# A two-stack transformer kernel: steps of the second stack's mixer placed between the tiles of its input projection

## The reference

```python
hx = modulate(rmsnorm_2(xs, mix_norm[l]), m_x, 1)
hc = modulate(rmsnorm_2(cs, mix_norm[l]), m_c, 1)
px = hx @ w_in[l]
if last:
    pc_kv = hc @ w_in[l][:, OFF_KV:]
else:
    pc = hc @ w_in[l]
    pc_kv = pc[..., OFF_KV:]
...
f = fourier_mix(proj[..., OFF_F:OFF_CB])                # fft2 over tokens and 64 channels, real part
cv = conv_mix(proj[..., OFF_CB:OFF_CC], proj[..., OFF_CC:OFF_CX], proj[..., OFF_CX:OFF_Q], conv_w)
...
kv_lat, k_rope = p_kv[..., :KV_LORA], p_kv[..., KV_LORA:]
kv = (rmsnorm_2(kv_lat, kv_norm) @ w_ukv).reshape(b, n, MLA_HEADS, QK_NOPE + V_DIM)
...
q = (rmsnorm_2(q_lat, q_norm) @ w_uq).reshape(b, n, MLA_HEADS, QK_NOPE + QK_ROPE)
```

## Time and profile before

| | |
|---|---|
| median of three runs | 2722.24 us |
| the profiled execution: its time | 2721.82 us |
| the profiled execution: its span | 2720.0 us |
| TensorE, VectorE, ScalarE busy | 2507.4, 1846.3, 1099.7 us |
| projection of layer 0, tiles 3 to 13 | 1350 to 1410 us |
| mixer of layer 0 | 1410 to 1443 us |
| projection of layer 1, tiles 3 to 13 | 2347 to 2390 us |
| mixer of layer 1 | 2390 to 2408 us |

### The profile page before, as it was taken

One profiled execution on the slowest core, in us unless ns is written; L12 is line 12 of the kernel. 1 busy time (PEld: TensorE's weight loads), 2 busy tenths in 40 slices (PEclk: granted clock), 3 DMA queues, 4 the chain that ended last, 5 costly groups with the idle time before them and its releaser, 6 DMA issues.

```text
span 2720.0 us, 37566 instructions
## 1 busy us (share of the span) xinstructions
PE 2507.4 (92%) x15010; PEld 2147.0 (79%) x15010; DVE 1846.3 (68%) x3136; ACT 1099.7 (40%) x1695; POOL 53.3 (2%) x56
## 2 busy tenths in 40 slices
PE   5889999866899799999987899999999999978998
PEld 4849999754799778888875588888888888866997
DVE  2647999644566667787945677676876666866666
ACT  4475447722454532222514452222442222544543
POOL 1010000021000000000000000000000000000000
PEclk8999999988999899999998999999999999988999
DMA  7877996522466546655322036555445554422663
GB/s 260 244 227 202 282 279 181 155 93 78 129 183 186 148 124 171 176 164 166 101 51 72 8 98 166 155 163 157 138 133 157 140 151 124 120 76 60 182 185 109
DMA packets 632563, 407.59 MB, mean 150 GB/s; under 512 B 27751, under 2 KB 588614, under 8 KB 631366
## 3 DMA queue, kind: packets, MB, share of 16 engines
q1 hardware_dynamic: 631712, 404.94, 51.8%
q10 hardware_dynamic: 678, 0.25, 0.0%
HBM read 404.09 MB, written 1.05 MB: 149 GB/s over the span
## 4 chain that ended last, share of the span: by engine, by line
PE 83%; DVE 8%; ACT 4%; DMA 2%; issue 1%; SPq 1%; ACTq 0%; POOL 0%; DVEq 0%; POOLq 0%
PE ps L1562 71%; PE ps L1584 2%; PE ps L1599 1%; PE ps L569 1%; PE ps L833 1%; DMA raw<-in_attn_w_in 1%; PE ps L1336 1%; DVE w_lo L1900 1%; PE ps L843 1%; PE ps L1311 1%; DVE p L1405 1%; DVE stat L1395 1%; DVE tmp L2100 0%; PE ps L1323 0%; DVE ada_acc L1917 0%
## 5 line engine op out<-in xcount | busy, mean ns | idle before, releaser
L1742 ACT CAST w_hi<-raw 128x1024 fp32r<-128x1024 f32 (+3 forms) x557 | 554.7, 997 | 1210.4 <-PE ps L1562 1174.0
L1562 PE MATMUL ps<-h_hi,w_hi 128*128 128x258 f32 (+2 forms) x2952 | 969.4, 328 | 27.2 <-DVE h_lo L2109 13.7
L1562 PE MATMUL ps<-h_lo,w_hi 128*128 128x258 f32 (+2 forms) x2952 | 964.5, 327 | 0.0
L1562 PE MATMUL ps<-h_hi,w_lo 128*128 128x258 f32 (+2 forms) x2952 | 963.6, 326 | 0.0
L1900 DVE TENSOR_TENSOR w_lo<-raw,w_hi 128x1024 fp32r<-128x1024 f32 (+3 forms) x557 | 644.9, 1158 | 256.9 <-ACT w_hi L1742 253.9
L1562 PEld LDWEIGHTS ps<-h_hi,w_hi 128*128 128x128 f32 x2952 | 561.3, 190 | 82.5 <-issue 26.5
L1562 PEld LDWEIGHTS ps<-h_lo,w_hi 128*128 128x128 f32 x2952 | 560.8, 190 | 46.7
L1562 PEld LDWEIGHTS ps<-h_hi,w_lo 128*128 128x128 f32 x2952 | 561.2, 190 | 45.4
L1562 PE MATMUL ps<-a_hi,w_hi 128*128 128x256 f32 (+1 forms) x1056 | 354.6, 336 | 0.5 <-DVE a_lo L1955 0.5
L1562 PE MATMUL ps<-a_lo,w_hi 128*128 128x256 f32 (+1 forms) x1056 | 353.2, 334 | 0.0
L1562 PE MATMUL ps<-a_hi,w_lo 128*128 128x256 f32 (+1 forms) x1056 | 353.2, 334 | 0.0
(11 more groups left out here) (350 smaller groups left out, 2249.0 us busy)
## 6 DMA issues: line engine op xcount, KB each, us to landing
raw<-in_ffn_w_in SPq DMA_DIRECT2D x264, 512.0 KB, 4.6
ada_raw<-in_w_mod SPq DMA_DIRECT2D x120, 512.0 KB, 3.9
raw<-in_ffn_w_out SPq DMA_DIRECT2D x96, 512.0 KB, 5.0
ada_raw<-in_ada_w SPq DMA_DIRECT2D x40, 512.0 KB, 5.4
wide_rows<-in_ada_w SPq DMA_DIRECT2D x40, 512.0 KB, 5.0
raw<-in_ffn_w_out SPq DMA_DIRECT2D x48, 384.0 KB, 3.6
raw<-in_gdn_w_in SPq DMA_DIRECT2D x33, 512.0 KB, 4.1
raw<-in_w_in SPq DMA_DIRECT2D x26, 512.0 KB, 3.9
```

Of the source, the lines that this page charges most:

```text
L1562: last = mm(ps[0:m, slot, 0:n], w[:, slot, k * P:k * P + m], v[:, s0 + k, c0:c0 + n], start=(k == 0 and w is w_hi and v is hi), stop=(k == ...
L1742: nc.scalar.copy(w_hi[:, slot, 0:n], raw[:, slot, 0:n]).then_inc(s_hi, 1)
```

## The change

`MIXER_STEPS` lists for each layer the order of the 14 tiles and behind which tile each mixer step stands; the results still go to the same blocks of `proj2`. The query latents (8, 9, 10) come first in both layers. In layer 0 the key-value latents and the key follow (11, 12, 13), in layer 1 four more tiles of one stream, then those three, then the last four. The mixer's functions become steps (`mixer_step_tensor`, `mixer_step_scalar`, `mixer_step_vector`) called inside the loops over the tiles; on VectorE the step stands ahead of the result copy of its tile, on ScalarE behind the cast and the epilogue. The squares move from VectorE to ScalarE; `fm` gets four buffers instead of two. Behind the last tile stay: the second convolution's gate, the splits of the mixed rows into two parts, and the later half of the token passes. In layer 1 the norm of the query latent and that of the key-value latent now have a logarithm and exponential each, where one pair of table loads served both.

```diff
+MIXER_STEPS = (
+    dict(order=(8, 9, 10, 11, 12, 13, 0, 1, 4, 6, 2, 5, 7, 3), kv=3, kr=5, f=6, q_sums=6, kv_sums=6, q_rstd=7, kv_rstd=7,
...
+    dict(order=(8, 9, 10, 0, 1, 4, 6, 11, 12, 13, 2, 5, 7, 3), kv=7, kr=9, f=3, q_sums=5, kv_sums=10, q_rstd=6, kv_rstd=11,
...
+        parts = ((0, 7, T), (7, 10, 2 * T), (10, 14, T)) if layer else ((0, 14, 2 * T),)
         st += [("norm", "both", ("mla", layer), 2 * T),
-               Linear("mixer_in", ("w_in_2", layer), KD, 11, own, loads=loads[:11], first=0, early="h"),
-               Linear("mixer_in", ("w_in_2", layer), KD, 3, 2 * T, loads=loads[11:], first=11),
+               *(Linear("mixer_in", ("w_in_2", layer), KD, b - a, n, loads=[loads[i] for i in order[a:b]], first=a, early=None if a else "h")
+                 for a, b, n in parts),
...
+            if t == at_["turn"]:
+                pe.wait_ge(s_evac, g0 + at_["kr"] + 1)
+                pe.wait_ge(event("latent_rstd"), 2 * layer + 1)
+                mm(ps[:, 7, 0:T], const("swap2"), proj2[:, 13, 0:T], start=True, stop=True).then_inc(event("k_rotated"), 1)
+            if t == 12:
+                for i in range(n_s):
+                    fourier_tokens(pe, layer, i)
+            if t == 13:
+                pe.wait_ge(event("latent_rstd"), 2 * layer + 2)
+                pe.wait_ge(event("k_roped"), layer + 1)
+                for i in range(n_s, 2 * n_s):
+                    fourier_tokens(pe, layer, i)
...
+        def mixer_step_scalar(act, lin, t):
...
+            if t in latent_squares(layer):
...
+                nc.scalar.activation(sq[:, e % 2, 0:n], proj2[:, at_["order"][t], 0:n], ACT.Square).then_inc(event("latents_squared"), 1)
+            sums = [("q_rstd", n_s * T, 384, ssq, 7, 1), ("kv_rstd", 2 * T, 256, rstd, 6, 2)]
+            sums = [s[1:] for s in sums if at_[s[0]] == t]
+            for n, width, r, bank, count in sums:
+                act.wait_ge(event("latent_sums"), 2 * layer + count)
+                last = nc.scalar.activation(r[:, 0:n], ps[:, bank, 0:n], ACT.Ln, scale=1.0 / width, bias=const("eps"))
...
+                    if lin.kind == "mixer_in":
+                        mixer_step_tensor(pe, lin, lin.more["first"] + j)
...
-                elif st[0] == "mixer":
-                    mixer_tensor(pe, st)
```

More of the change, by code:

```diff
@@ L1184, in mixer_scalar @@
[L1184 to L1191, removed]
@@ L1202, in latent_parts, with conv_out @@
-        def latent_parts(n_s):
[L1204 to L1208, removed]
+            hi = mixed_rows(st)[0]
+            act.wait_ge(s_tile, tiles_before(st))
+            def conv_out(f):
+                act.wait_ge(event("conv_mixed"), 2 * layer + f + 1)
+                nc.scalar.copy(hi[:, 2 + f, 0:n_s * T], cv[:, f, 0:n_s * T]).then_inc(event("conv_hi"), 1)
@@ L1212, in mixer_vector @@
             layer, n_s = st[1], 2 - st[1]
-            tokens = n_s * T
-            b, nb = 4 * mixer_base(st), 2 * mixer_base(st)
+            hi, lo = mixed_rows(st)
             dve.wait_ge(s_evac, tiles_before(st))
[L1217 to L1224, removed]
@@ L1277, in mixer_vector, with conv_lo @@
-            last.then_inc(s_h, 4 * n_s)
+            conv_gated(layer, 1)
+            for k in range(*MIXER_STEPS[layer]["parts"].get(13, (0, 0))):
+                latent_lo(dve, layer, k)
+            dve.wait_ge(event("conv_mixed"), 2 * layer + 2)
+            def conv_lo(f):
+                dve.wait_ge(event("conv_hi"), 2 * layer + f + 1)
+                return V.tensor_tensor(lo[:, 2 + f, 0:n_s * T], cv[:, f, 0:n_s * T], hi[:, 2 + f, 0:n_s * T].bitcast(F32), ALU.subtract)
+            conv_lo(0)
@@ L1422, in mla_vector @@
                     V.tensor_tensor(mixed_rows(st)[1][d], ps[:, 6 + b % 2, 0:T], mixed_rows(st)[0][d].bitcast(F32), ALU.subtract).then_inc(s_h, 1)
-        def lat_blocks(lin):
-            i = next(n for n, s in enumerate(stages) if s is lin)
-            total = 0
-            for s in stages[:i]:
-                if not isinstance(s, Linear) and s[0] == "mixer":
-                    total += 4 + 3 * (1 if s[1] else 2)
-            return total
         block = stack.enter_context(nc.Block())
@@ L1620, in waits @@
                 if src == "lat":
-                    total = lat_blocks(lin)
+                    layer = lin.weight[1]
+                    total = 10 * layer + 3 * (2 - layer) + (4 if lin.kind == "key_value" else 0)
                     return lambda k: (event("lat_written"), total)
@@ L1808, in _ @@
                         epilogue(st, j)
+                        if st.kind == "mixer_in":
+                            mixer_step_scalar(act, st, st.more["first"] + j)
                         norm, late = late_parts(st, j)
@@ L2152, in _ @@
                             angles()
+                        if st.kind == "mixer_in":
+                            mixer_step_vector(dve, st, st.more["first"] + j)
                         epilogue(st, j)
```

218 lines of the change are left out of this document (123 added, 95 removed).

## The result

| | before | changed |
|---|---|---|
| median, timed side by side | 2723.19 us (2720.78 to 2724.53, four runs) | 2698.79 us (2694.61 to 2701.40, four runs) |
| the same in a later comparison | 2723.65 us (2720.77 to 2726.34, nine runs) | 2698.87 us (2697.87 to 2701.49, four runs) |
| profiled execution: span, time | 2720.0, 2721.82 us | 2699.6, 2701.36 us |

A forecast was written before the change was run, and what follows sets the result against it. TensorE, carrying 83% of the chain that ended last, was taken as the bound. Layer 0's 22.4 us plus layer 1's 0.5 make 22.9 off the median 2722.24: 2699.3, rounded 2699 us, range 2693 to 2705.

The forecast's parts named there:

- Layer 0, 22.4 us: Layer 0's gain: query 20.1 us sooner plus 2.3 us from the full clock; bounds 20 to 23.5.
- the breaks: Cost of small steps interrupting projection matmuls: 0.1 us each, 7 in layer 0 and 6 in layer 1; bounds zero and 0.2.
- The wait ahead of tile 7, 8.6 us: Layer 1: TensorE waits 8.6 us for the last normed blocks before the first tile of both streams.
- ScalarE's detour: Layer 1: two table loads, a logarithm and an exponential ahead of the last two h_hi; without their cost, wait 6.5 us.
- The low clock behind it, 2.0 us: Layer 1: after the wait TensorE runs at the lower clock level for a while, losing 1.8 to 2.6 us, taken as 2.0.
- Query 54 us after tile 4: Layer 1: from tile 4 to the first query matmul takes 54 us, the query starting at 2407.7, as before.
- Layer 1, plus 0.5 us: Layer 1's gain: 0.8 us at the query tiles less some 0.3 for breaks; bounds a 2.5 loss to a 5 gain.
- The table loads: ScalarE: each load counted as 1.28 us without drain; the skill's 2.66 us would lengthen the wait by 2.8, giving 2702.
- layer 1 did not pay: Rival 1: tile 7's wait does not form or stays short, layer 1 gives 12 us, time 2688; chance 0.06.
- rival 2: New waits cost more than counted: layer 0 gives 20 us, layer 1 loses 3, time 2705; chance 0.17.
- layer 0 lost nothing in its tail: Rival 4: layer 0's last convolution and mixed-row splits hold the query back by 8 us, time 2707; chance 0.05.
- the full grant held for 70 us: Rival 3: a lower clock throughout the interleaved stretches makes the kernel slower than before, 2732; chance 0.03.

The follow-up runs named there:

- l1_only: Layer 1 as in the changed kernel, layer 0 as in the kernel before: 2723.26 us, ratio 1.0003 to the kernel before.
- l0_conv_tail: Changed kernel with layer 0's second convolution (3.0 us of VectorE) moved from under the last projection tile to behind it: 2701.01 us, ratio 0.9918.
- busy: Changed kernel with 17 matmuls, whose results nothing reads, filling TensorE's wait ahead of layer 1's tile 7: 2698.57 us, ratio 0.991.
- shift1_late: Changed kernel with one more one-stream tile ahead of layer 1's two-stream tiles, and the query norm's logarithm and exponential one tile later: 2693.99 us.
- shift2: Changed kernel, layer 1's two-stream tiles two places later, query norm's logarithm and exponential later, last two key-value latent parts behind the last tile: 2694.27 us.
- shift1: Changed kernel with one more one-stream tile and its feature pass ahead of layer 1's first two-stream tile: 2694.38 us, ratio 0.9891.
- l0_only: Layer 0 as in the changed kernel, layer 1 with the old tile order and old mixer: 2702.13 us, ratio 0.9925.
- changed_again: The changed kernel timed once more, beside later variants: 2698.87 us.

## Why the prediction was right, point by point

The places and causes were right. That the time was hit to 0.2 us is luck: layer 0 gave 0.5 us more than forecast and layer 1 some 0.6 us less, the two misses cancel, and medians with an interval of 5 us to either side could not have told 2699 from 2695 or 2703.

- **Layer 0, 22.4 us.** Measured 22.9 (126.51 to 103.58), and 126.45 in `l1_only` for 102.96 to 103.92 in the nine executions with the new order. The query was to come 20.1 us sooner and came 20.7 sooner. The step that was too large is the breaks, 0.1 us each: eleven tiles of 5.445 us (four of them from 1352.27 to 1374.05) are 59.9, the steps 12.5, together 72.4 of the 72.43 measured. The row of the first query matmul starts some 0.2 us early (0.41 us ahead of the next, where the later ones are 0.23 apart), so the seven breaks cost up to 0.2 us in all, where 0.7 was counted. The clock's 2.3 us held: query to rotation took 31.15 for 33.34.
- **No wait in layer 0.** Right, with 3.9 us of room, and 1.9 with 3 us more of VectorE in the tail (`l0_conv_tail`).
- **The wait ahead of tile 7, 8.6 us.** Measured 8.37 to 8.39. Both parts were right in kind: taking ScalarE's detour away leaves 6.47, where 6.5 was written as the bound without it.
- **The low clock behind it, 2.0 us.** It was 2.5 (`busy`), and 2.3 to 2.5 in the four executions with this order against the 5.53 us that tile 7 takes at the full clock: the upper end of the 1.8 to 2.6 given. This is the term that was mis-sized. The low level lasted up to 5.25 us (2351.60 to 2356.85), where 3.6 to 5.2 had been read from the kernel before.
- **Query 54 us after tile 4.** 54.45, 54.21, 54.42 and 54.40 us in four executions; the forecast was 0.2 to 0.5 too low, which is about what that term lacks. The 0.5 us of wait at query tile 3 was there (0.53).
- **Layer 1, plus 0.5 us.** In the profiled execution it was 1.1 us of loss. The other three executions with this order give 77.27 to 77.86 us, for 77.47 and 77.96 with the old one: on the mean 0.1 us of loss, so neither gain nor loss can be told. Of the 1.6 us missing in the profiled execution, half a microsecond is the clock term. The other step that failed is that the loads behind the mixer follow "at the same pace". The wait ahead of the rotation was 2.40 us before and 3.52 after: the last key-value results stand on VectorE behind weight parts of the output projection, these behind casts, and these behind loads. `l1_only`, whose wait was 2.40 us as before, took 77.27 us, 0.2 less than before. ScalarE in the changed kernel:

```profile
2404.31 1.05 ACT L1783 CAST w_hi<-raw 128x1024 fp32r<-128x1024 f32 x1 [1.21 <-DMA raw<-in_w_out]
2406.92 1.05 ACT L1783 CAST w_hi<-raw 128x1024 fp32r<-128x1024 f32 x1 [1.56 <-DMA raw<-in_w_out]
```

and VectorE:

```profile
2408.01 1.23 DVE L1943 TENSOR_TENSOR w_lo<-raw,w_hi 128x1024 fp32r<-128x1024 f32 x1 [0.78 <-ACT w_hi L1783]
2409.15 0.68 DVE L2086 COPY kv<-ps 128x512 f32<-128x512 f32 x1
```

Over both layers of the eleven profiled executions this wait was 2.40 to 2.81 us with the old order (four times, mean 2.6) and 2.40 to 3.52 with the new one (eighteen times, mean 2.9). That the query tiles now run into these loads sooner fits it, but the scatter of one order is as large as the difference, and no run held the loads apart, so this cause is argued and not shown.
- **The table loads.** The activation behind a load of 1.28 us starts 0.01 us after it, twice in the rows above (0.02 in the earlier trace rows), and the load itself starts 0.02 us behind the cast ahead of it, so no drain stands on either side. The Trainium skill, "ScalarE: Activation LUTs", section "What ACT_TABLE_LOAD costs", would add 1.38 us of drain to each; the wait would then be 11 us, and it is 8.4. The 1.28 us of the trace decide.
- **The rivals.** None came whole: layer 1 did not pay, of rival 2 only the low level of 5 us came, layer 0 lost nothing in its tail, and the full grant held for 70 us with seven groups of small steps in it.

## What to carry to other kernels

Work moved from a tail into a stretch where the bounding engine is full costs its own length there and saves the whole chain of the tail; count the engines that make the inputs of the tiles whose order changes with it, for a reordering can bring a hidden producer to the front. In such a place each microsecond taken off the new wait pays until the next queue shows, here the weight parts behind VectorE's tail, so look at what the other engines still do behind the last tile before trying for more.

## What the hardware showed

- **A short idle time lowers the clock too, and after a delay.** After 2.72 us without work (`shift1_late`) TensorE came back at the full clock, 0.23 us from the second matmul to the third, and then fell to 1.2 GHz, some 0.43 us apart, for eight of them:

```profile
2350.24 0.47 PE L1604 MATMUL ps<-h_hi,w_hi 128*128 128x512 f32 x1 [2.72 <-DVE h_lo L2154]
2350.55 0.41 PE L1604 MATMUL ps<-h_hi,w_lo 128*128 128x512 f32 x1
2350.78 0.61 PE L1604 MATMUL ps<-h_lo,w_hi 128*128 128x512 f32 x1
2351.19 0.63 PE L1604 MATMUL ps<-h_hi,w_hi 128*128 128x512 f32 x1
...
2354.18 0.42 PE L1604 MATMUL ps<-h_hi,w_lo 128*128 128x512 f32 x1
2354.43 0.39 PE L1604 MATMUL ps<-h_lo,w_hi 128*128 128x512 f32 x1
```

  The same happened after 3.45 us in `shift2`. The low level cost 2.3 to 2.5 us after 8.4 us of idle time, 1.7 after 6.47 us, and 2.0 and 1.6 after 4.65 and 2.72 us (the three wide tiles took 18.4 and 18.05 us, for 16.4 in `shift2`, which did not wait there). So the price fell much less than the wait did. After 1.24 us of idle time at tile 4, and 1.37 us at query tile 3 of `shift1`, there was no low level at all.
- **Breaks between matmuls of different kinds are nearly free**: seven in layer 0 cost up to 0.2 us in all.
- **The same program scatters, and its granted clock with it.** The part ahead of layer 0's projection is equal in all kernels, and tile 3 began between 1349.5 and 1356.3 us in eleven executions. In the slowest (`l0_only`) the mean grant was 0.86 from 100 to 200 us and 0.93 from 700 to 800, in the fastest (`changed_again`) 0.90 and 0.97, with TensorE's longest waits there the same within 1 us. What made the grant differ is not shown. A change of 2 us is therefore to be read from its stage and not from the time.
